# Gated linear attention: the two heads of a pair innermost in the order of its small matrix products

## The reference, cut to what matters

```python
b = jnp.cumsum(log_a, axis=-2)
q_dec = q * jnp.exp(b)
k_inv = k * jnp.exp(-b)
k_end = k * jnp.exp(b_last - b)
a = jnp.where(mask, jnp.einsum('bhncd,bhnsd->bhncs', q_dec, k_inv), 0.0)
o = jnp.einsum('bhncs,bhnse->bhnce', a, v)
ds = jnp.einsum('bhncd,bhnce->nbhde', k_end, v)
...
return o + jnp.einsum('bhncd,nbhde->bhnce', q_dec, s_prev)
```

## Time and profile before

| | |
|---|---|
| median of three runs | 1690.85 us |
| profiled execution, its own time | 1686.82 us |
| its span | 1685.0 us |
| PE busy | 1579.1 us, 94% |
| VectorE, ScalarE, GpSimd busy | 50%, 37%, 33% |
| mean granted clock of TensorE | 0.944 |

### The profile page before, as it was taken

One profiled execution on the slowest core, in us unless ns is written; L12 is line 12 of the kernel. 1 busy time (PEld: TensorE's weight loads), 2 busy tenths in 40 slices (PEclk: granted clock), 3 DMA queues, 4 the chain that ended last, 5 costly groups with the idle time before them and its releaser, 6 DMA issues.

```text
span 1685.0 us, 20836 instructions
## 1 busy us (share of the span) xinstructions
PE 1579.1 (94%) x8734; PEld 1337.0 (79%) x8734; DVE 848.6 (50%) x1081; ACT 629.9 (37%) x1008; POOL 564.1 (33%) x231
## 2 busy tenths in 40 slices
PE   4979989989799999998899998999988999999996
PEld 4978878879699999976668865777876888888885
DVE  3233033341788888854459947874355334432122
ACT  4451053373443333322342235344544323333221
POOL 2321011104144444443504432321442434444441
PEclk9989589969899999999979999999998999999998
DMA  4211012102122222566512321211221333332332
GB/s 174 88 51 39 13 38 85 40 12 89 42 96 88 88 98 91 187 227 233 202 43 94 100 73 42 74 51 38 95 81 63 125 112 105 109 125 88 105 107 75
DMA packets 43628, 155.32 MB, mean 92 GB/s; under 512 B 4848, under 2 KB 5488, under 8 KB 43536
## 3 DMA queue, kind: packets, MB, share of 16 engines
q1 hardware_dynamic: 42960, 151.51, 26.6%
q10 hardware_dynamic: 576, 2.49, 0.4%
HBM read 151.89 MB, written 2.10 MB: 91 GB/s over the span
## 4 chain that ended last, share of the span: by engine, by line
PE 82%; DVE 7%; ACT 6%; DMA 3%; issue 2%; SPq 0%; POOL 0%; DVEq 0%; ACTq 0%
PE G L410 69%; DMA raw<-wstream 2%; DVE ada_acc L1714 2%; PE G L552 2%; PE B L859 1%; PE B L387 1%; PE B L879 1%; PE G L645 1%; PE B L771 1%; PE B L604 1%; PE G L546 1%; ACT whi L956 1%; PE G L647 1%; PE B L621 1%; PE B L530 1%
## 5 line engine op out<-in xcount | busy, mean ns | idle before, releaser
L367 POOL TENSOR_TENSOR wlo<-raw,whi 128x1024 fp32r<-128x1024 f32 x227 | 563.9, 2488 | 1092.9 <-ACT whi L956 1092.7
L410 PE MATMUL G<-uhi,whi 128*128 128x258 f32 (+4 forms) x1920 | 542.0, 335 | 37.1 <-DVE ulo L1439 12.3
L410 PE MATMUL G<-ulo,whi 128*128 128x258 f32 (+4 forms) x1920 | 530.2, 329 | 0.0
L410 PE MATMUL G<-uhi,wlo 128*128 128x258 f32 (+4 forms) x1920 | 528.8, 328 | 0.0
L410 PEld LDWEIGHTS G<-uhi,whi 128*128 128x128 f32 x1920 | 327.9, 194 | 104.0 <-issue 67.0
L410 PEld LDWEIGHTS G<-uhi,wlo 128*128 128x128 f32 x1920 | 328.6, 194 | 30.1
L410 PEld LDWEIGHTS G<-ulo,whi 128*128 128x128 f32 x1920 | 328.8, 194 | 27.9
L956 ACT ACTIVATE whi<-raw 128x1024 fp32r<-128x1024 f32 x227 | 239.4, 1055 | 224.1 <-DMA raw<-wstream 224.0
L410 PE MATMUL G<-yhi,whi 128*128 128x512 f32 x352 | 141.8, 403 | 12.8 <-POOL wlo L367 12.8
L410 PE MATMUL G<-yhi,wlo 128*128 128x512 f32 x352 | 140.8, 400 | 0.0
L410 PE MATMUL G<-ylo,whi 128*128 128x512 f32 x352 | 140.8, 400 | 0.0
(11 more groups left out here) (266 smaller groups left out, 1646.9 us busy)
## 6 DMA issues: line engine op xcount, KB each, us to landing
raw<-wstream SPq DMA_DIRECT2D x227, 512.0 KB, 3.3
ada_in<-ada SPq DMA_DIRECT2D x40, 512.0 KB, 5.5
ada_late<-ada SPq DMA_DIRECT2D x8, 512.0 KB, 3.8
h<-hT SPq DMA_DIRECT2D x8, 264.0 KB, 4.8
out<-res SPq DMA_DIRECT2D x8, 256.0 KB, 2.2
biasn<-bias SPq DMA_DIRECT2D x2, 960.0 KB, 11.0
biasn<-bias ACTq DMA_DIRECT2D x2, 960.0 KB, 5.6
scan_keep<-scanm SPq DMA_DIRECT2D x1, 528.0 KB, 8.7
```

The source lines that it names most:

```text
L367: pool.tensor_tensor(wlo[:, i, :], raw[:, i, :], whi[:, i, :].bitcast(F32), ALU.subtract)\
L410: ins = pe.matmul(dst[:, x, 0:xw], w[:, slot, b * P:(b + 1) * P], u[:, k, off + x0:off + x0 + xw], start=(first and i == 0 and j == 0), st ...
```

## The change

In the scores the loop over `par` becomes the innermost, so that each product is followed by one on the other half of the rows. In the values the loop over `hp` is outside: both heads of a pair make their full product one after the other, and then the small products take the two heads in turn. The products, their operands, their destinations, the waits and the signals are the same, and so is their number; within each PSUM region the order of accumulation is the same.

```diff
-                for par in range(2):
-                    bank = 2 * (i % 2) + par
-                    for d in range(2):
-                        for hp in range(2):
-                            last = pe.matmul(B4[0:n, bank, (2 * d + hp) * P:(2 * d + hp) * P + n],
-                                             kinv[par * DK:(par + 1) * DK, 2 * d + hp, t0:t0 + n],
-                                             qdec[par * DK:(par + 1) * DK, 2 * d + hp, t0:t0 + n],
-                                             start=True, stop=True)
+                for m in range(4):
+                    for par in range(2):
+                        last = pe.matmul(B4[0:n, 2 * (i % 2) + par, m * P:m * P + n],
+                                         kinv[par * DK:(par + 1) * DK, m, t0:t0 + n],
+                                         qdec[par * DK:(par + 1) * DK, m, t0:t0 + n], start=True, stop=True)
                 last.then_inc(s["a_ps"], 1)
...
-                for par in range(2):
-                    for hp in range(2):
+                for hp in range(2):
+                    for par in range(2):
                         hh = 2 * hp + par
                         pe.matmul(G[:, 1, par, hp * P:hp * P + n], vgl[0:n, i, hh * DV:(hh + 1) * DV],
                                   Amat[0:n, i % 2, (2 * par + hp) * P:(2 * par + hp) * P + n],
                                   start=True, stop=False)
-                        for x, c in enumerate(chunks):
-                            cn, ct = chunk_place(c)[2:]
-                            for d in range(2):
+                    for x, c in enumerate(chunks):
+                        cn, ct = chunk_place(c)[2:]
+                        for d in range(2):
+                            for par in range(2):
                                 last = pe.matmul(G[:, 1, par, hp * P + x * CHUNK:hp * P + x * CHUNK + cn],
                                                  S[par * DK:(par + 1) * DK, d, c, hp, :],
                                                  qdec[par * DK:(par + 1) * DK, 2 * d + hp, ct:ct + cn],
```

## The result

The changed kernel takes 1652.26 us (median of four, 1651.10 to 1654.86), the kernel before 1689.78 (four runs, 1687.84 to 1692.06): ratio 0.978, 95% interval 0.9761 to 0.9798, 37.5 us less. The forecast was 1668 with a range from 1658, 23 us less. The sign was right, the size too small by 40%. Two executions further down, of 2526 and 2498 us, ran at a clock of 0.55 throughout and are left out of every comparison.

A forecast was written before the change was run, and what follows sets the result against it. PE alone was taken to bound the scores-and-values stage, busy for all 61.70 us. Scores 2.8 plus values 16.3 make 19.1 us; with 4 for the clock, 23 us off 1690.85 gives 1668 us, range 1658 to 1677.

The forecast's parts named there:

- PE alone sets the time of the stage: Scores and values: PE busy for all of 61.70 us, so each microsecond saved moves the stage's end.
- Two streams on the two row halves: Scores and values: two streams of eight records run side by side in 1.03 us at the upper clock.
- Who is late next: In the stage VectorE and ScalarE stay hidden; after it ScalarE sets the end, pieces 26 and 27 giving at most 0.44 us.
- The clock: In the stage, shorter value blocks keep PE's clock up somewhat more, worth 4 us beyond the gain at unchanged levels.
- 19.1 of unchanged levels: Scores 2.8 us plus values 16.3 us saved, at the clock that each unit had before.
- own bound of 33 us: Scores, values and pieces: if the clock stayed up throughout, the stage would take 28.5 us, 33 less.
- Rival A: In the stage the clock stays up nearly throughout: 30 us saved, 1661; chance 0.15.
- B: In scores and values streams run side by side only in part: 10 us saved, 1681; chance 0.05.
- C: In scores and values each change of half costs 0.17 to 0.26 us: slower, 1703 to 1711; chance 0.015.
- D: The stage's gain is given back in the neighbourhood attention, where PE waits for VectorE; chance 0.015, shared with no effect.

The follow-up runs named there:

- grouped order: Changed kernel, but in the values the small products of a pair of heads go all of the upper half first, then all of the lower; 1662.43 us.
- added products: Kernel before with two useless dense products between heads in each value block, thirty in all; 1696.42 us, ratio 1.0041.
- runs of two: Changed kernel with the halves alternating after every two products instead of after each, in scores and values; one run, 1659.01 us.
- half-filler kernel: Kernel before with one useless dense product between heads in each value block, fifteen in all; 1684.11 us, ratio 0.998.
- four quarters: Changed kernel with forward and backward products of the state sums in turn, on opposite row halves, column halves still alternating; 1650.89 us, ratio 0.9789.
- both orders: Changed kernel with the state sums in all four quarters of the array and, in values, small products first, full products last; 1649.66 us, ratio 0.9769.

## Why the prediction was wrong, point by point

- *PE alone sets the time of the stage*: right. 28.61 of 28.61 us busy, and the 33.1 us come out one for one.
- *Two streams on the two row halves*: right, in each term. Expected and measured: scores 1.08 and 1.09 us, full products of a pair 0.64 and 0.64, sixteen small ones 1.03 and 1.04, a value block 3.34 and 3.37, the small block 2.2 and 2.19. The 0.11 us a record, which the author took with 0.13 as the bound, came out: two full records more take 0.64 - 0.42 = 0.22 us. The grouped order shows that the alternation does it (1.53 us). These are the terms at the upper clock; those at the lower (1.95 and 3.04) were never met, as the clock stayed up.
- *Who is late next*: right. No wait of PE in the stage; the end passes to ScalarE with 0.44 us.
- *The clock*: the term that failed. "I take the 19.1 of unchanged levels and somewhat under a third of the 14 us between it and 33, 4 us: 23 us." All 14 came: 28.5 us was worked out for a clock that stays up, 28.61 was measured. The 10 us that the forecast left out are the stage's 33.1 less its 23.
- *What lay beyond the range* was more than this term. The text's own bound of 33 us gives 1657.8, the lower end of the range; the other 5.5 us down to 1652.26 are 1.1 by which the median before fell with its fourth run, 1.8 between profiled runs and medians, 1.2 from before the stage, 0.4 at the `sg` copy and 1.1 from later. Most of this is scatter, which the text had put at 3 to 4 us.
- The reason given for the small share was the false step: "the new products keep the array's columns busy only a little more of the time", with the falls after 2.9 us of values as evidence. These falls were at the old rate of ten records in 1.45 us; the new passes twenty in 1.68, 70% more work in the same time at the same clock. I had priced the overlap in time and not in what it does to the clock. The trace calls PE busy for all of the stage in both kernels, at 0.63 and at 1.00, so the profile's busy share does not tell them apart. The added products show the same: busy for 68.30 of 68.30 us, clock 1.00.
- *Rival A* (the clock stays up, 30 us, 1661) had 0.15 and was the mechanism. It too was short, by 3 us in the stage and by what lies before and behind it; its 30 was under the 33 of the same text's own bound.
- B, C and D fell: halves alternating at every product are the fastest (1.04 us, against 1.09 with runs of two and 1.53 with runs of four); a change of half at every product left sixteen records at 1.04 us where eight without one take 1.03; and 34.6 us are still there at the first product of the neighbourhood attention.
- How much of the 33.1 us is clock can now be said another way. The half-filler kernel does the old order at the upper clock: 56.00 us less fifteen added products of 1.05, plus twelve times 0.20 (in the first four blocks the full product behind one takes 0.22 and not 0.42), is about 43 us. So the old order at the upper clock would have 43, the clock is worth about 19 us and the order about 14 at the upper clock. This sum is worked out, no kernel ran it alone. The 19.1 and 14 us of the forecast split the same 33 otherwise: first the order at the levels that the clock had, then what the clock gives on top.

## What to carry to other kernels

Where small products use half of the array's rows or columns, put products of different halves next to each other: here two streams of eight records took 1.04 us where one took 1.03, and four streams of six took 1.03. The products of the two row halves went into different banks in the scores, the values and the four quarters, and the same bank was not tried; those of the two column halves (L515) went into one bank and ran side by side all the same, sixteen records in 1.02 us. Where PE is busy throughout and its clock is low all the same (61.70 of 61.70 us, 0.63), and a change packs its work closer, reckon the whole stretch at the upper clock as a case of its own, pieces between included, and let the range reach it. A gain of a few us in one stage can be lost again later (with both orders 4.9 us at the end of the stage, 1.0 in the span); look for it in the stage, and in the median only with its interval.

## What the runs showed that was not expected

- Useless products can make a kernel faster: 15 x 1.05 us added, 4 us off the median, as the clock rose from 0.63 to 1.00 in the stage.
- An fp32 product of 512 columns takes 1.05 us as a pair of records (1.91 us for two in a row), where the projections' `float32r` products of 264 columns take 0.12 to 0.14 us, one record each; the filler was mis-sized by this.
- Four streams in the four quarters of the array: sixteen records in 0.60 us, 24 in 1.03.
- Products of the other half start before the first half's are through (4 records in the first 0.55 us of the old score block, 9 in the next 0.35); runs of two cost 5 to 9% (1.09 for 1.04 us, 1.19 for 1.09) and runs of four some 50% (1.53 for 1.04, 1.64 for 1.09).
- Which measure of the work the clock goes by was not settled here; the number of records is not it (6.4 a microsecond with the added products, all at 1.00; 7.5 in the old order's thin stretches, in which it fell), and neither is the profile's busy share (all of the stage at 0.63 and at 1.00).
